# First MLP's up product by seven block products in two phases, with the w_ada rows weighted from buffers of their own

## The reference, cut to what matters

```
h  = h + mixed @ w_out
hn = rms_norm(h, norm_mlp_w)
h  = h + square(relu(hn @ w_up)) @ w_down        # w_up 1024 x 4096, w_down 4096 x 1024
...
mod = silu(c) @ w_ada + b_ada                    # third block; w_ada 1024 x 6144, c one vector
```

## Time and profile before

| | |
|---|---|
| median of 3 runs | 3478.18 us (3473.32 to 3481.44) |
| span of the profiled execution | 3475.1 us |
| PE busy | 3418.8 us (98%) |
| DVE / ACT / POOL busy | 1586.9 / 983.6 / 1220.9 us |
| chain that ended last, share of PE | 94% |
| HBM read / written | 222.40 / 18.00 MB |

### The profile page before, as it was taken

The page is one execution under the profiler, slowest core; times in us unless marked ns, Lnnn a source line. Parts: engine busy times, 40 slices in busy tenths (PEclk is TensorE's granted clock), DMA queues, the critical chain, the costliest instruction groups (busy, mean ns, idle before and its releaser), DMA issues.

```text
span 3475.1 us, 39075 instructions
## 1 busy us (share of the span) xinstructions
PE 3418.8 (98%) x16826; PEld 2784.5 (80%) x16826; DVE 1586.9 (46%) x1671; ACT 983.6 (28%) x1441; POOL 1220.9 (35%) x646
## 2 busy tenths in 40 slices
PE   8999999999999999999999999999999999999998
PEld 6887888888888878765788888888888788888887
DVE  5553343333333558486545445445645531222224
ACT  5432221111111221385332222222333432222222
POOL 3112324444444223413323344444322343333333
PEclk9999999999999999999999999999999999999999
DMA  3112312222222311210211222222211111111113
GB/s 111 37 49 70 118 49 79 87 83 91 91 88 91 100 67 49 79 60 1 79 49 49 74 91 82 79 94 73 95 43 43 67 56 49 49 49 49 49 49 127
DMA packets 89431, 242.93 MB, mean 70 GB/s; under 512 B 13334, under 2 KB 20262, under 8 KB 89132
## 3 DMA queue, kind: packets, MB, share of 16 engines
q1 hardware_dynamic: 89260, 240.44, 19.9%
HBM read 222.40 MB, written 18.00 MB: 69 GB/s over the span
## 4 chain that ended last, share of the span: by engine, by line
PE 94%; DVE 3%; ACT 2%; POOL 1%; issue 0%; DMA 0%; POOLq 0%; SPq 0%; DVEq 0%; ACTq 0%
PE ps L618 29%; PE ps L621 28%; PE ps L619 28%; PE ps L790 1%; PE ps L1028 1%; PE ps L1077 1%; PE ps L648 1%; PE ps L1061 1%; PE ps L650 1%; PE ps L649 1%; DVE P L2356 1%; ACT T L1619 0%; PE ps L1014 0%; PE ps L992 0%; PE ps L981 0%; PE ps L686 0%
## 5 line engine op out<-in xcount | busy, mean ns | idle before, releaser
L2736 POOL TENSOR_TENSOR wlo<-raw,whi 128x1024 fp32r<-128x1024 f32 (+3 forms) x367 | 697.1, 1900 | 1728.5 <-ACT whi L1299 1728.5
L618 PE MATMUL ps<-HH,whi 128*128 128x512 f32 (+2 forms) x2736 | 1080.1, 395 | 6.4 <-POOL HL L2742 3.1
L619 PE MATMUL ps<-HL,whi 128*128 128x512 f32 (+2 forms) x2736 | 1069.3, 391 | 0.0
L621 PE MATMUL ps<-HH,wlo 128*128 128x512 f32 (+2 forms) x2736 | 846.9, 391 | 0.0
L1299 ACT ACTIVATE whi<-raw 128x1024 fp32r<-128x1024 f32 (+3 forms) x367 | 309.7, 844 | 1618.4 <-PE ps L621 1419.8
L618 PEld LDWEIGHTS ps<-HH,whi 128*128 128x128 f32 (+2 forms) x2736 | 513.0, 187 | 118.5 <-POOL HL L2742 3.5
L621 PEld LDWEIGHTS ps<-HH,wlo 128*128 128x128 f32 (+2 forms) x2736 | 512.7, 187 | 112.2 <-issue 0.6
L619 PEld LDWEIGHTS ps<-HL,whi 128*128 128x128 f32 (+2 forms) x2736 | 512.9, 187 | 108.9 <-issue 2.0
L618 PE MATMUL ps<-GH,whi 128*128 128x512 f32 x1512 | 594.3, 393 | 0.6 <-POOL wlo L2736 0.6
L619 PE MATMUL ps<-GL,whi 128*128 128x512 f32 x1512 | 588.4, 389 | 0.0
L621 PE MATMUL ps<-GH,wlo 128*128 128x512 f32 x1512 | 466.1, 389 | 0.0
(11 more groups left out here) (386 smaller groups left out, 2929.2 us busy)
## 6 DMA issues: line engine op xcount, KB each, us to landing
raw<-in_w_up SPq DMA_DIRECT2D x76, 512.0 KB, 3.2
raw<-in_w_in SPq DMA_DIRECT2D x70, 512.0 KB, 3.2
raw<-in_w_fc SPq DMA_DIRECT2D x64, 512.0 KB, 3.2
raw<-in_w_down SPq DMA_DIRECT2D x104, 256.0 KB, 2.6
raw<-in_w_ada SPq DMA_DIRECT2D x48, 512.0 KB, 3.3
raw<-in_w_fc SPq DMA_DIRECT2D x64, 256.0 KB, 2.6
X<-in_xT SPq DMA_DIRECT2D x16, 512.0 KB, 7.1
raw<-in_w_out SPq DMA_DIRECT2D x16, 512.0 KB, 3.2
```

Of the source, the lines that this page charges most:

```text
L618: e.matmul(o_[0:m, half(hf)], whi_[:, k, :], hi[k0 + k][:, half(hf)], start=first, stop=False)
L619: e.matmul(o_[0:m, half(hf)], whi_[:, k, :], lo[k0 + k][:, half(hf)], start=False, stop=False)
L621: i = e.matmul(o_[0:m, half(hf)], wlo_[:, k, :], hi[k0 + k][:, half(hf)], start=False, stop=last)
L2736: e.tensor_tensor(wlo_of(name), raw_of(name), whi_of(name).bitcast(F), SUB).then_inc(*po.inc("lo " + name))
```

## The change

**Up phase.** All of w_up comes first. Two row tiles (2n and 2n + 1), the two halves of the input features and the two halves of the tokens make a 2 x 2 block product. It is done with seven products instead of eight, the Strassen-Winograd form, in the order of PARTS. Each product is 4 k x 3 matmuls of 512 columns. Its token operands OH/OL are sums and differences of blocks of the weighted X, made once ahead of and during the first pair. Its weight operands are sums and differences of the four half tiles, made by DVE for each pair (`fast_sums`, four half-width operations: s5, s7, s6, s3), then copied by ACT to a ring of four half-width buffers WH and reduced to their low parts by POOL. The products accumulate in four PSUM banks, partly on top of each other (p2 on p1, p7 on p6, p3 on p5); DVE adds the corners together in SBUF while it drains them, and ACT squares. The hidden tiles don't stay in SBUF: SP stores each to a buffer hsc in HBM.

**Down phase.** 32 jobs follow, four groups of eight, each over 8 k (48 matmuls). The hidden tiles of the next group are read back from hsc one a job, ACT makes the high and POOL the low part. The first eight are read back at the end of the up phase.

**w_ada.** Its tiles leave the list. They are loaded by SP into three buffers AR (T[1], RT, T[0]), two in each of the first 24 down jobs, weighted by POOL and summed by DVE and PE as before.

The diff, cut to its core:

```diff
-ADA_AT = sorted([n for n in range(4, 88) if (n - 4) % 12 in (0, 1, 2, 5, 7, 9)] + [15, 27, 39, 51, 63, 75])
+ADAS = [[2 * n, 2 * n + 1] if n < 24 else [] for n in range(32)]
+
+PARTS = ("p1", "p5", "p6", "p4", "p7", "p2", "p3")
...
-    mlp("w_up", "w_down", "up", "dn", [4] * 8, aux=[(f"ada{m}", d["w_ada"][m]) for m in range(48)], aux_at=ADA_AT)
+    for m in range(32):
+        plan(f"up{m}", d["w_up"][m])
+    for n in range(32):
+        g, m = divmod(n, 8)
+        plan(f"dn{g}_{m}", d["w_down"][m, :, 1024 * g:1024 * g + 1024])
...
+        AR = [T[1], RT, T[0]]
+        TX, RL = unit("TX", GO, 15, [P, S]), at("RL", RO, [P, S], R)
+        HF, GF = unit("HF", HO, 8, [P, 8, S]), unit("GF", GO, 8, [P, 8, S])
...
+            def fast(t, n, ready=None, between=None):
+                bx, bz, by, bw = corners(t, n)
+                bank = {"p1": bx, "p2": bx, "p5": bz, "p3": bz, "p6": by, "p7": by, "p4": bw}
+                for j, p in enumerate(PARTS):
+                    w = 7 * n + j
+                    q.wait_ge(*po(f"{t}lo {n} {p}"))
+                    if p == "p2":
+                        q.wait_ge(*ac(f"{t}s {n}"))
+                    elif p == "p7":
+                        q.wait_ge(*dv(f"{t}u2 {n}"))
+                    elif p == "p3":
+                        q.wait_ge(*dv(f"{t}c22a {n}"))
+                    elif n:
+                        q.wait_ge(*dv({"p1": f"{t}c11a {n - 1}", "p5": f"{t}c12a {n - 1}", "p6": f"{t}u3 {n - 1}", "p4": f"{t}c21a {n - 1}"}[p]))
+                    wh, wl_ = WH[w % 4][:].rearrange("p (k m) -> p k m", k=4), part(t, n, p)[1].rearrange("p (k m) -> p k m", k=4)
+                    for k in range(4):
+                        if between:
+                            between(p, k)
+                        if ready:
+                            for tok in ready(p, k):
+                                q.wait_ge(*tok)
+                        e.matmul(bank[p], wh[:, k, :], OH[p][:, k, :], start=k == 0 and p not in ("p2", "p7", "p3"), stop=False, skip_group_check=True)
+                        e.matmul(bank[p], wh[:, k, :], OL[p][:, k, :], start=False, stop=False, skip_group_check=True)
+                        i = e.matmul(bank[p], wl_[:, k, :], OH[p][:, k, :], start=False, stop=k == 3, skip_group_check=True)
+                    freed_ = {"p2": pair_of(t, n)[:1], "p7": pair_of(t, n)[1:]}.get(p, ())
+                    i.then_inc(*pe.inc(f"{t}{n} {p}", *freed_))
...
+            for n in range(16):
+                fast("up", n, ready=None if n else ready2, between=norm2 if n == 1 else None)
+            for n in range(32):
+                g, j = divmod(n, 8)
+                if (g, j) == (3, 0):
+                    lend("n3 sq")
+                job(f"dn{g}_{j}", ghs if g % 2 else hhs, gls if g % 2 else hls, lambda k: [either(f"dnl {8 * g + k}")], 8)
+                row_step(n)
             row_step(-1)
...
+            def fast_hi(t, w, *tok):
+                n, p = w // 7, PARTS[w % 7]
+                a, b = pair_of(t, n)
+                if p in ("p1", "p2"):
+                    q.wait_ge(*dma[f"w{widx[a] % 4}"](a))
+                elif p == "p4":
+                    q.wait_ge(*dma[f"w{widx[b] % 4}"](b))
+                else:
+                    q.wait_ge(*dv(f"{t}s{p[1]} {n}"))
+                for x in tok:
+                    q.wait_ge(*x)
+                if w > 3:
+                    q.wait_ge(*pe(f"{t}{(w - 4) // 7} {PARTS[(w - 4) % 7]}"))
+                e.activation(WH[w % 4][:], part(t, n, p)[0], ACT.Copy).then_inc(*ac.inc(f"{t}hi {n} {p}"))
...
-            mlp("up", "dn", [4] * 8, "n2", [pe("wo7")], after=after_row, on_last=on_last3)
+            for n in range(32):
+                g, j = divmod(n, 8)
+                highs(widx[f"dn{(n + 1) // 8}_{(n + 1) % 8}"] if n < 31 else widx["gg0"])
+                if g < 3:
+                    f = 8 * g + 8 + j
+                    k = 8 * (1 - g % 2) + j
+                    high(f"dnh {f}", (HF if g % 2 else GF)[:, j, :], (HH if g % 2 else GH)[:, j, :], dma[f"hr{k}"](f"hr {f}"))
+                elif j:
+                    on_last3(j - 1)
+            on_last3(7)
...
+            def fast_step(t, n, p, relu, last=False):
+                bx, bz, by, bw = corners(t, n)
+                ha, hb = hidden(n)
+                q.wait_ge(*pe(f"{t}{n} {p}"))
+                if p == "p6":
+                    q.wait_ge(*ac(f"{t}s {n}"))
+                    if n > 1:
+                        q.wait_ge(*dma[f"h{2 * (n % 2)}"](f"{t}h {2 * n - 4}"))
+                    tt(ha[:, half(1)], hb[:, half(1)], by, ADD, f"{t}u2 {n}")
+                elif p == "p2" and not n:
+                    copy(ha[:, half(0)], bx, f"{t}c11a {n}")
+                elif p == "p2":
+                    finish(ha[:, half(0)], bx, 0, relu, f"{t}c11a {n}", f"{t}c11 {n}")
+                elif p == "p7":
+                    tt(hb[:, half(0)], hb[:, half(1)], by, ADD, f"{t}u3 {n}")
+                    q.wait_ge(*dv.now())
+                    tt(hb[:, half(1)], hb[:, half(0)], bz, ADD, f"{t}c22a {n}")
+                    if n:
+                        fast_end(t, n, "c22", relu)
+                elif p == "p4":
+                    tt(hb[:, half(0)], hb[:, half(0)], bw, ADD, f"{t}c21a {n}", *([f"free {t} yw"] if last else []))
+                    if n:
+                        fast_end(t, n, "c21", relu)
+                elif p == "p3":
+                    tt(ha[:, half(1)], ha[:, half(1)], bz, ADD, f"{t}c12a {n}", *([f"free {t} xz"] if last else []))
+                    if n:
+                        fast_end(t, n, "c12", relu)
...
+            for n in range(16):
+                if 1 < n < 15:
+                    fast_sums("up", n + 1)
+                fast_step("up", n, "p6", True)
+                if n == 0:
+                    for i in range(4):
+                        low_operand("p2", i)
+                elif n == 15:
+                    low_down(1)
+                    low_down(3)
+                fast_step("up", n, "p7", True)
+                if n == 0:
+                    fast_sums("up", 1)
+                fast_step("up", n, "p2", True)
+                if n == 0:
+                    low_operand("p3", 2)
+                    low_operand("p3", 3)
+                    square_sum("n2", 7)
+                elif n == 15:
+                    low_down(5)
+                fast_step("up", n, "p4", True, last=n == 15)
+                fast_step("up", n, "p3", True, last=n == 15)
+                if n == 0:
+                    fast_sums("up", 2)
+                    factors("n2")
+                    q.wait_ge(*ac("n2 rt"))
+                    for c in ("c22", "c11", "c21", "c12"):
+                        fast_end("up", 0, c, True)
+            low_down(7)

...
-                if n in ADA_AT:
-                    f = ADA_AT.index(n)
-                    row_sum(f"ada{f}", f, *([pe(f"row{f - 2}")] if f > 1 else []))
+
+                for f in ADAS[n]:
+                    q.wait_ge(*po(f"ada{f}"))
+                    if f > 1:
+                        q.wait_ge(*pe(f"row{f - 2}"))
+                    e.tensor_reduce(adat[:, f % 2, :], AR[f % 3][:].rearrange("p (k m) -> p m k", k=8), AX.X, ADD).then_inc(*dv.inc(f"red ada{f}"))
...
-            mlp("up", "dn", [4] * 8, "n2", "dn x", on_last3, step=row_step)
+            for n in range(32):
+                g, j = divmod(n, 8)
+                if g:
+                    q.wait_ge(*dv(f"dn x{g - 1} {j}"))
+                to_x(f"dn{g}_{j}", j, f"dn x{g} {j}")
+                row_step(n)
+                if g == 3 and j:
+                    on_last3(j - 1)
+            on_last3(7)
...
+            for w in range(7, 112):
+                if w == 109:
+                    lows(widx["dn0_0"])
+                fast_lo("up", w)
+            for k in (0, 2, 4, 6):
+                low(f"dnl {k}", HF[:, k, :], HH[:, k, :], HL[:, k, :], ac(f"dnh {k}"))
...
-            def row_step(n, name):
-                if n in ADA_AT:
-                    f = ADA_AT.index(n)
-                    row_tile(f"ada{f}", SC[:], ac("sc"))
-                    lows(widx[name] + 3)
-
-            mlp("up", "dn", [4] * 8, row_step)
-
+            for n in range(32):
+                g, j = divmod(n, 8)
+                lows(widx[f"dn{(n + 1) // 8}_{(n + 1) % 8}"] if n < 31 else widx["gg0"])
+                if g < 3:
+                    low(f"dnl {8 * g + 8 + j}", (HF if g % 2 else GF)[:, j, :], (HH if g % 2 else GH)[:, j, :], (HL if g % 2 else GL)[:, j, :], ac(f"dnh {8 * g + 8 + j}"))
+                for f in ADAS[n]:
+                    w_ = AR[f % 3][:].rearrange("p (k m) -> p k m", k=8)
+                    q.wait_ge(*dma[f"ar{f % 3}"](f"ada{f}"))
+                    q.wait_ge(*ac("sc"))
+                    tt(w_, w_, SC[:].unsqueeze(2).broadcast_to([P, 8, P]), MUL, f"ada{f}")
...
+            def spill(t, n, hf):
+                q.wait_ge(*ac(f"{t}sq {2 * n + hf}"))
```

(120 more changed lines are left out.)

173 lines of the change are left out of this document (147 added, 26 removed).

## The result

The changed kernel takes 3546.6 us (median; 3545.2 to 3548.6), the kernel before 3476.1 us in the same measurement: ratio 1.0204, 95% interval 1.0189 to 1.0218. The direction was forecast, the size was not: 3501 us with a range up to 3535.

The account below looks back on a forecast made before the run. TensorE, busy 98% of the span, was taken to bound the kernel. 3475.1 - 43.5 (up product) + 11 (start) + 55 (down loop) = 3497.6, plus 3.1 to the runs' median: 3501 us; own range 3486 to 3520, reaching to 3471 and 3535.

Parts of the forecast that it names:

- Up product: Up phase: 1344 matmuls instead of 1536, 192 fewer at 0.2267 us each, saving 43.5 us.
- Steady up phase: Up phase after its start: the other engines' additions fit behind TensorE's matmuls, costed at nothing.
- The hole of 1.6 us at pair 15: Change from up to down phase: product p3 may wait 0.3 us for ScalarE's copies; nothing added.
- Start: Start of the up phase: late low parts for p3 of pair 0 and late u2 in pair 1, +11 us (5 to 16).
- The rule about VectorE and Pool: Start of up phase: Pool and a two-SBUF-input VectorE operation lock each other out; first pair ends nearer 27 than 24 us.
- the additions before the third product and in p4 are just hidden: Start of up phase, pair 0: these additions cost TensorE no wait, unlike those for p3.
- The loop: Down jobs with w_ada: read-back, high part, low part, weightings, reduction, row load; 13.8 us against 11.4, +55 us (32 to 78).
- 4.1 to land: Landing term of the down-phase turn: a read-back takes 4.1 us with a row load right ahead; bounds 3.1 and 5.1.
- rival (c): Down phase: longer turn from a third transfer ahead or falling clock; 14.8 us gives 3524; 0.14 together with slower products.
- First read-back at S + 8: Down phase, counted from S, the start of its first job: first read-back at about 8 us, tile 1 reduced at 21.7.
- (a): Down phase keeps TensorE's pace, turn at most 11.4 us: 3446 us; chance 0.15 including what lies between it and (b).
- (b): Down phase: same loop, read-back landing as if alone, turn 12.8 us, loss 32: 3478 us, no change; chance 0.11.

Follow-up runs that it names:

- e1: Changed kernel with SP issuing the next hidden tile's read-back ahead of a down job's two w_ada loads, not behind the second reduction: 3459.5 us.
- e11: Changed kernel with one w_ada load issued 0.37 us ahead of the read-back, the other load and the weight tile behind its landing: 3523.6 us.
- the two cuts: The runs e1 and e2, each a reordering of one queue of the changed kernel: 3459.5 and 3459.0 us.
- the dose: Changed kernel with ScalarE making the high part of each tile read back in the down phase twice: 3570.7 us.
- e2: Changed kernel with Pool's two w_ada weightings of a down job ahead of the low part of the hidden tile read back: 3459.0 us.
- e10: Changed kernel with SP issuing the read-back alone and waiting for it to land before the job's w_ada loads and weight tile: 3491.8 us.

## Why the prediction was right in direction and wrong in size

- **Up product, -43.5 us.** Right. The steady part has 245.39 busy of 246 us, the pace is 0.227 us a matmul, and these matmuls are the only work of TensorE that e1 has less than the kernel before, which it beats.
- **Steady up phase at nothing.** Right, for pairs 2 to 14. The hole of 1.6 us at pair 15 was put at 0.3.
- **Start, +11 us (5 to 16).** Mis-sized: 21.6 us for the whole up phase. 11.9 us are holes behind the start, 1.3 and 1.6 those at w_out's end and at pair 15; the rest, some 7 us, is mostly the lower clock behind them (0.91 to 0.93 from 478 to 540 us), which I left out: in e11, with no more idle time and 0.78 from 477 to 540 us, the up phase is some 6 us longer again. The rule about VectorE and Pool was used for single operations; in pair 0 it sets the price of all of them, and "the additions before the third product and in p4 are just hidden" left out p7.
- **The loop, 13.8 us a turn.** The mechanism was right in every link, shown by the chain, by the two cuts and by the dose. The term that failed is "4.1 to land, because a row load is right ahead of it". It measured 5.67 (mean 5.63); with 0.1 less on the others that is 15.2 a turn, and 23 x 1.4 = 32 of the 46 us between 3501 and 3546.6. Two loads ahead alone make it 5.2 by e2's mean; the weight tile behind goes with the rest. The case stood in rival (c) as "a third transfer ahead", priced 14.8, though the loop as written out has the third transfer: tile 2n + 3 is loaded 1.9 us before tile 2n + 4, 2.2 us before the read-back.
- **First read-back at S + 8.** It went out at S + 12.0 (818.06), since VectorE's last drains of pair 15 waited behind low parts and Pool longer than counted. Tile 1 was reduced at S + 27.0: 5 us more.
- **Rivals.** (a) did not happen, but e1 and e2 show that in another order of the same operations TensorE does set the pace: 3459 us, 13 above (a)'s 3446, most of it the dearer start. (b) is e10, a read-back that lands as if alone: 12.6 us a turn as (b) had it, 3492 us with the dearer start and the later first read-back. The clock of (c) did fall, to 0.90, and cost little in the loop: PE was busy 299.4 us there and idle 55, and no link of the turn shown is PE's.
- **The range** reached to 3535 by a turn of 14.8. With both upper bounds together, 78 for the loop and 16 for the start, the sum is 3529. It had nothing for what came on top: a turn of 15.2, a first read-back 4 us later, and a start that cost more than its bound.

## What to carry to other kernels

Where work is handed round several in-order queues, look for a path that comes back to its own start, and compare one turn with the work it should hide behind; average load says nothing (ScalarE was 13% busy and each of its microseconds counted). Such a loop is cheap to cut: one line of order in either of two queues was worth 87 us here. Price a transfer by everything in flight between its issue and its landing, not by its neighbour ahead alone; loads issued behind it may belong to it too. And compare single runs by the stretch that was changed: two executions of the same code ahead of it were up to 10 us apart here.

## What the runs showed of the hardware

A 512 KB read into SBUF on SP's queue reached its reader after 3.24 us alone (mean of the down phase 3.4), 4.2 to 4.5 (4.6) with one like it issued 0.37 us ahead, 5.0 to 5.4 (5.2) with another 1.9 us before that, 6.1 (6.4) with three ahead. In the changed kernel, where 512 KB follow 0.49 us behind it, it took 5.67 (5.6), and e1 took 5.1 to 5.5 (5.4) with one load 0.37 us ahead and one 2.9 us behind. Reading a buffer that the kernel had written or an input made no difference. Half-width operations of VectorE with two inputs in SBUF (0.68 to 0.75 us alone) and of Pool (1.29) took 1.70 and 1.72 us when both engines had a row of them. In the down jobs with w_ada tiles TensorE had 38 idle gaps, 1.5 us long on average and 3.2 at most, and its granted clock averaged 0.90.
